# A loop over five head pairs in place of five written-out copies, on TensorE and ScalarE

## The reference, cut to what matters

```
def step(S, inp):
    r_t, w_t, k_t, v_t, kk_t, a_t = inp
    s_kk = einsum('zbhvk,zbhk->zbhv', S, kk_t)
    S = S * w_t - s_kk * (kk_t * a_t) + v_t * k_t
    return S, einsum('zbhvk,zbhk->zbhv', S, r_t)
...
y = (y - mu) * rsqrt(var + GN_EPS) * gn_w + gn_b
out = (y + bonus) * gate
```

## Time and profile before

| what | value |
|---|---|
| median of 3 runs | 2577.07 us (2575.86 to 2584.42) |
| the profiled execution's own time | 2571.64 us |
| its span | 2569.8 us |
| PE / PEld / DVE / ACT / POOL busy | 91 / 61 / 70 / 48 / 6% of the span |
| instructions recorded | 50155 |
| head stage, from the first pair's first product to the sixth's gating | 221.2 to 930 us of the span |
| queue q8, kind "instruction" | 116 packets, 1.90 MB |
| queue q14, kind "instruction" | 52 packets, 0.43 MB |

### The profile page before, as it was taken

The page is one execution under the profiler, slowest core; times in us unless marked ns, Lnnn a source line. Parts: engine busy times, 40 slices in busy tenths (PEclk is TensorE's granted clock), DMA queues, the critical chain, the costliest instruction groups (busy, mean ns, idle before and its releaser), DMA issues. The chain is left out here.

```text
span 2569.8 us, 50155 instructions
## 1 busy us (share of the span) xinstructions
PE 2330.2 (91%) x18800; PEld 1560.3 (61%) x18800; DVE 1807.5 (70%) x2317; ACT 1235.5 (48%) x1499; POOL 157.4 (6%) x160
## 2 busy tenths in 40 slices
PE   5987898989898789699999999899896999999996
PEld 2444676767676765466666666555454666666665
DVE  2344676766676622799999999389317999999994
ACT  2021323232323211578888888202215887888882
POOL 1000000000000000000000000000000000000000
PEclk8998999999999999899999999999998999999999
DMA  9953010101010022799999998501007999999993
GB/s 355 350 188 138 4 31 3 31 3 31 3 31 19 3 92 92 271 380 387 383 388 388 384 389 320 187 1 66 1 24 272 377 391 384 387 388 389 383 386 93
DMA packets 176362, 539.25 MB, mean 210 GB/s; under 512 B 12417, under 2 KB 48897, under 8 KB 176066
## 3 DMA queue, kind: packets, MB, share of 16 engines
q1 hardware_dynamic: 169666, 514.63, 52.2%
q0 software_dynamic: 6528, 22.29, 3.7%
HBM read 510.29 MB, written 26.61 MB: 209 GB/s over the span
## 5 line engine op out<-in xcount | busy, mean ns | idle before, releaser
L1941 DVE TENSOR_TENSOR wl<-raw,wh 128x1024 fp32r<-128x1024 f32 x768 | 897.2, 1222 | 75.3 <-DVEq L1940 66.9
L1883 ACT ACTIVATE wh<-raw 128x1024 fp32r<-128x1024 f32 x768 | 795.8, 1058 | 233.2 <-ACTq L1882 225.1
L1816 PE MATMUL ps<-wh,xs 128*80 128x512 f32 x3072 | 843.8, 393 | 4.3 <-PEq L1811 4.3
L1816 PEld LDWEIGHTS ps<-wh,xs 128*80 128x80 f32 x3072 | 449.3, 148 | 242.9 <-issue 4.6
L1816 PE MATMUL ps<-wl,xs 128*80 128x512 f32 x1536 | 476.2, 391 | 0.0
L1816 PEld LDWEIGHTS ps<-wl,xs 128*80 128x80 f32 x1536 | 227.1, 148 | 126.8
L1445 DVE COPY_PREDICATED wk<-m,ps 128x512 f32<-128x512 uint8 x180 | 130.9, 732 | 102.6 <-DVEq L1444 101.8
L772 PE MATMUL ps<-h,wk 128*128 128x512 f32 (+1 forms) x576 | 176.6, 448 | 3.1 <-PEq L1043 3.1
L1165 ACT ACTIVATE wk<-ps 128x256 f32<-128x256 f32 (+1 forms) x180 | 65.8, 366 | 195.0 <-ACTq L1164 194.7
L772 PEld LDWEIGHTS ps<-h,wk 128*128 128x128 f32 x576 | 94.3, 193 | 77.5 <-issue 74.7
L2060 PE MATMUL ps<-h,wk 128*128 128x512 f32 (+1 forms) x448 | 122.0, 434 | 3.3 <-PEq L2051 3.3
(11 more groups left out here) (284 smaller groups left out, 2690.1 us busy)
## 6 DMA issues: line engine op xcount, KB each, us to landing
raw<-in_moe_w_gate SPq DMA_DIRECT2D x64, 2048.0 KB, 10.4
raw<-in_moe_w_up SPq DMA_DIRECT2D x64, 2048.0 KB, 11.7
raw<-in_moe_w_down SPq DMA_DIRECT2D x64, 2048.0 KB, 11.4
wk<-in_mod_w SPq DMA_DIRECT2D x24, 2048.0 KB, 10.8
wk<-in_ev_w_in SPq DMA_DIRECT2D x18, 512.0 KB, 5.2
wk<-in_od_w_in SPq DMA_DIRECT2D x4, 2048.0 KB, 15.8
ysum<-raw SPq DMA_DIRECT2D x10, 512.0 KB, 17.1
hrow<-rows SPq DMA_DIRECT2D x10, 512.0 KB, 4.9
```

The lines of the kernel that those rows point to most:

```text
L1816: last = pe.matmul(ps[0:CAP, b0 + k], lhs[:, xk, c, :], w[:, s, a:b], start=c == 0 and xk == 0 and w is wh, stop=c == KC - 1 and xk == 1)
L1883: act.activation(wh[:, n % SPLIT], raw[:, n // 4 % RAW, n % 4], ACT.Copy).then_inc(sem("high_ready"), 1)
L1941: dve.tensor_tensor(wl[:, n % SPLIT], raw[:, n // 4 % RAW, n % 4], wh[:, n % SPLIT].bitcast(F32), ALU.subtract).then_inc(sem("low_ready"), 1)
```

## The change

The five copies of `heads(True)` become one body in a loop, on TensorE and on ScalarE. The sixth pair, `heads(False)`, stays as it is, as do the programs of VectorE, GpSimd and SyncE. `Fori` emits a MOVE ahead of the loop, and an ALU_OP and a COMPARE_BRANCH at the end of each turn; no more than that is added, and nothing of the body is changed.

```diff
                     mod_turn(pe, PARTS - EARLY)
                     pe.wait_ge(sem("mod_read"), 1).then_inc(sem("mod_read"), -1)
                     slot_read(2)
-                    for i in range(HP - 1):
+                    with pe.Fori(0, HP - 1) as i:
                         heads(True)
                     heads(False)
...
                     act.activation(ysq, rkv[:, VV], ACT.Square).then_inc(act_done, 1)
                     done("ysq_ready")
-                    for i in range(HP - 1):
+                    with act.Fori(0, HP - 1) as i:
                         heads(True)
                     heads(False)
```

## The result

The changed kernel takes 2597.43 us (median of 8 runs, 2590.19 to 2601.93), the kernel before 2575.72 us on the same chip (median of 8). The ratio is 1.0083, with a 95% interval of 1.007 to 1.0096: slower by 21.7 us. (All medians are of fast runs; one of the ten of e3, 4193.6 us at a granted clock of 0.735, is left out.) The profiled execution has a span of 2595.9 us, 26.1 more than the one before.

A forecast was written before the change was run, and what follows sets the result against it. No engine is full; each pair is a chain between PE, DVE and ACT, so uncovered PE stalls delay the end. Block waits 15.6 plus clock 1.7 gave +17.3 us: 2577.07 + 17.3 = 2594.4 us, full range 2577 to 2602.

The forecast's parts named there:

- Part 1: At the joint between pairs: the loops' added instructions, 0.24 us per turn on TensorE, are covered and cost nothing.
- Part 2: TensorE's branch back waits 3.99 us for the head's program block; mostly covered, shifting the joint 0.65 to 1.0 us.
- Part 3: Behind the loop's head: TensorE waits for a second block; shift 3.9 us per turn, 15.6 us over four branches.
- Part 4: TensorE's clock drops after the joint's idle times: 1.7 us in all, ends 0 and 6.8.
- Part 5: Inside the pairs: q8's packets, their spacing and the stalls stay; the shorter program saves no time.
- One block, not two: Rival, chance 0.27: at each joint only the first block's wait counts; +3 to +5 us, 2581 us.
- Nothing to wait for: Rival, chance 0.09: TensorE's body or head stays in the engine, or no loop is kept; 2577 us.
- ScalarE too: Rival, chance 0.09: ScalarE's loop body doesn't stay either, delaying its copies at the joint; 2602 us.
- Faster: Rival, chance 0.05: fixed block boundaries make all four turns run like the shortest pair; 7.0 us gained, 2570 us.

The follow-up runs named there:

- e3: Kernel before with both loops, TensorE's loop head placed at the start of a 256-instruction block: 2592.42 us, ratio 1.0063 to the kernel before.
- e2: Kernel before with only ScalarE's five pairs in a loop, TensorE written out: 2571.72 us, ratio 1.0004.
- e5: Kernel before with both loops, TensorE's head at slot 128 of a 256-instruction block, no branch hint: 2587.12 us, ratio 1.0048.
- e7: Kernel before with both loops, TensorE's head at slot 235 as in the changed kernel, plus a branch hint: 2583.55 us, ratio 1.004.
- e9: Changed kernel plus four idle 512-column matmuls on TensorE ahead of the branch back: 2596.13 us, ratio 1.0088 to the kernel before.
- e10: Kernel before with a TensorE loop of two turns, the other three pairs and all of ScalarE written out: 2581.18 us, ratio 1.0025.
- e6: Kernel before with TensorE alone in a loop, head at slot 128, with a branch hint, ScalarE written out: 2583.47 us, ratio 1.0031.
- e8: Kernel before without any loop, each written-out pair's first TensorE instruction placed at a block's start: 2588.22 us, ratio 1.006.

## Why the prediction was right, and where not

The forecast was +17.3 us with a range of the whole kernel from 2577 to 2602; measured are +21.7 and 2597.43. Point by point:

- **Part 1, the added instructions cost nothing:** right. e2 shows it for ScalarE; on TensorE 36 + 76 ns remain where the branch falls through. That nothing else is added was wrong: the two table loads of 1.28 us in each joint were not foreseen. They found cover, and e2 shows no cost (23.88 us for a joint at full clock, as before).
- **Part 2, the branch waits for its block:** right. 3.3 to 3.8 us (once 4.8, in e5), where 3.99 was taken from the packets' spacing. It comes back in every run whose branch had no effective hint, and falls to 0.4 us with one.
- **Part 3, a second block 21 instructions on:** right in place and kind, and it is this that makes most of the cost. The stall comes behind ten weight loads, two matmul records into the second direction. e3 (head at a block's start) removes it and 18 of the 25 us in the joints; in e7 the block comes some 5 us earlier, and the wait for it is covered. The shifts measured in the four profiled joints are 4.2, 3.9, 4.7 and 3.4 us, 16.1 in all against 15.6 in the sum. That the two agree so closely is in part luck: of the two waits put at 3.99 each, the first took 3.4 to 3.9 us and the second 4.0 to 5.1.
- **Part 4, the clock:** the term that was mis-sized. I took half of a 1.7 us loss at two of four joints, 1.7 us in all. All four joints fall to half clock, for 6.8 to 10.2 us each, not 3.4. The joints' growth of 25.3 us less the 16.1 of the shifts leaves 9.1 us, some 2.3 per joint, where the sum has 0.4. The step that failed was to price a drop by the one stretch of 3.40 us seen behind a single wait, although here two waits follow each other with little work between them, and to count it at two joints of four. That the remainder is the clock is read from profiles: in e9 it falls to 1.6 us at each joint with one stretch and to 0.15 at the joint with none. The whole kernel's time does not show it, since e9's 3.6 us are too few to be told. The premise that the 2.02 us at the joint bring no drop holds for the four joints of before, but not always: in e2 two joints of four drop behind the same wait, and in e10 two of the three without a branch back.
- **Part 5, what stays:** right for this kernel, and in part by luck. The rests are no longer than before (386.8 us; 386.0 to 388.0 in the other runs with the head in this place; 389.0 and 385.5 for the place of before, in two executions). They would have been elsewhere: 391.5 and 392.6 with the head at slot 128, 396 to 399 at slot 0, looped or not. The prediction had no term for the place. It counted the head's place only for the joint.

Of the rivals, *One block, not two* is what the joints of e3, e5 and e6 show, where the head lies far from its block's end, and only there. *Nothing to wait for* is out, and in its place the Trainium skill's page "Runtime: NRT & Kernel Launch", section "Instruction fetch mechanics", is confirmed for TensorE: a body of 3.7 thousand instructions does not stay, and the taken branch stalls. *ScalarE too* is out: q14 brings 45 packets instead of 52, the seven blocks of 128 instructions of four bodies of 218 that are no longer in the program, and e2 costs nothing; so a body of 220 instructions stays, over at least two blocks of 8 KB. *Faster* had a real mechanism, but no gain came of it: fixed boundaries can move the kernel, and in the runs here they made it slower or left it as it was.

No version that was tried beats the kernel before. The best with all five pairs in TensorE's loop (e6, e7) cost 0.3 to 0.4%; ScalarE's loop alone (e2) costs nothing measurable.

## What to carry to other kernels

A loop whose body is longer than the engine holds pays at each branch back for the head's block, about 3.5 us here, and for a second one if the head lies near a block's end; whether this shows depends on what other engines do at that moment, so look for the wait that already stands at the joint and count how much of the body it covers. The place of a long body relative to its blocks is a variable of its own (2.5 us per turn between slots 235 and 0 in the loops, e3 against the changed kernel, and 1.8 without a loop, e8 against before), so an experiment that moves code should look at the stalls called "issue" in dense stretches before it blames the edit. A branch hint removes the wait only where it takes effect; check the COMPARE_BRANCH's duration.

## What was not expected of the hardware

- The clock: two idle times of some 3 and 2 to 4 us with 1 to 2 us of work between brought 6.8 to 10.2 us at half clock, each of four times. A single wait of 2.0 us at the joint brought none four times before, but a stretch at half clock that cost 1.6 us at two joints of four in e2.
- The hint took effect with the branch 144 and 123 instructions into its block (0.42 and 0.35 us), and not with 16 (3.60 us, medians).
- Placement: a block boundary at the end of the small matmuls stalls PE for 1.4 to 1.7 us in each of the five pairs of e8, and the rests of four turns are 396.2 to 399.2 us at slot 0 against 385.5 to 389.0 at the place of before and at slot 235. TensorE's program of before, unchanged, differs by 3.6 us between two executions (before and e2).
- Put into a loop, ScalarE's program has two table loads of 1.28 us in each turn (L1153 and L1146) where the written-out copies have one in all. This is in the program, not in the chip; why it comes was not looked into.
